# Token-tile steps interleaved at the joints of a fused two-block transformer kernel, one weight remainder moved to GpSimd, one clamp moved ahead of a split

## The reference

```python
ff = swiglu(rms_norm_2(h, g[0]), ffn_w_gate_up[i, 0], ffn_w_down[i, 0])
h = h + 0.5 * rms_norm_2(ff, g[1])
m_in = rms_norm_2(h, g[2])
mix = short_conv_mixer(...) if i == 0 else gated_deltanet_mixer(...)
h = h + rms_norm_2(mix, g[3])
ff = swiglu(rms_norm_2(h, g[4]), ffn_w_gate_up[i, 1], ffn_w_down[i, 1])
h = h + 0.5 * rms_norm_2(ff, g[5])
```

## Time and profile before

| | |
|---|---|
| median of three runs | 1706.47 us (1706.26 to 1706.6) |
| profiled execution: time | 1707.06 us |
| profiled execution: span, first to last instruction | 1705.1 us |
| mean granted TensorE clock | 0.963 of full |
| busy: TensorE, VectorE, ScalarE, GpSimd | 91%, 60%, 49%, 6% of the span |

### The profile page before, as it was taken

How to read it: one execution, slowest core, us unless ns; L and a number is a source line. 1 busy time by engine, 2 the same in 40 slices (tenths; PEclk the granted TensorE clock), 3 DMA queues, 4 the chain that set the end, 5 groups by cost and what they waited for, 6 DMA issues and landing times.

```text
span 1705.1 us, 19163 instructions
## 1 busy us (share of the span) xinstructions
PE 1554.3 (91%) x7536; PEld 1274.7 (75%) x7536; DVE 1022.7 (60%) x1345; ACT 832.8 (49%) x1174; POOL 96.0 (6%) x171
## 2 busy tenths in 40 slices
PE   4999889998999999899998999886688899989997
PEld 4777668777888778788877888764577778778886
DVE  3666566755665566666566565646655556766564
ACT  4535454463454454544455444554445645554443
POOL 4000000000000000000000000000422221000000
PEclk9899979999999999999999999988989999999999
DMA  4333433333555555555545555342322212455552
GB/s 157 121 98 124 123 100 114 99 121 109 191 186 184 173 181 177 164 184 183 191 158 182 179 192 191 123 132 72 87 56 75 75 50 75 154 163 189 192 179 99
DMA packets 165712, 238.77 MB, mean 140 GB/s; under 512 B 19358, under 2 KB 112328, under 8 KB 165624
## 3 DMA queue, kind: packets, MB, share of 16 engines
q1 hardware_dynamic: 154336, 230.98, 41.6%
q0 software_dynamic: 1632, 5.41, 1.1%
q10 hardware_dynamic: 9656, 1.18, 0.4%
HBM read 235.96 MB, written 1.57 MB: 139 GB/s over the span
## 4 chain that ended last, share of the span: by engine, by line
PE 70%; DVE 12%; ACT 8%; issue 5%; DMA 3%; POOL 1%; ACTq 1%; SPq 0%; DVEq 0%; POOLq 0%
PE A L226 12%; PE A L227 11%; PE A L228 11%; PE G L226 4%; PE G L228 4%; PE G L227 4%; PE M L228 4%; PE M L226 4%; PE M L227 4%; DVE w_lo L210 3%; ACT w_hi L197 2%; DVE gdn_gd_t L2274 2%; PE G L947 2%; PE G L989 1%; DMA raw<-in_w_mem_kv 1%
## 5 line engine op out<-in xcount | busy, mean ns | idle before, releaser
L210 DVE TENSOR_TENSOR w_lo<-raw,w_hi 128x2048 fp32r<-128x2048 f32 (+1 forms) x290 | 511.8, 1781 | 250.5 <-ACT w_hi L197 249.1
L197 ACT ACTIVATE w_hi<-raw 128x2048 fp32r<-128x2048 f32 (+1 forms) x290 | 424.5, 1483 | 206.6 <-DMA raw<-in_ffn_w_gate_up 151.5
L226 PE MATMUL A<-w_hi,x_hi 128*128 128x512 f32 (+3 forms) x688 | 291.9, 424 | 19.1 <-ACT gdn_gd_u L2048 9.6
L227 PE MATMUL A<-w_lo,x_hi 128*128 128x512 f32 (+3 forms) x688 | 270.6, 393 | 0.0
L228 PE MATMUL A<-w_hi,x_lo 128*128 128x512 f32 (+3 forms) x688 | 270.5, 393 | 0.0
L226 PEld LDWEIGHTS A<-w_hi,x_hi 128*128 128x128 f32 x688 | 138.8, 202 | 52.9 <-DVE x_lo L351 11.3
L228 PEld LDWEIGHTS A<-w_hi,x_lo 128*128 128x128 f32 x688 | 138.3, 201 | 27.8
L227 PEld LDWEIGHTS A<-w_lo,x_hi 128*128 128x128 f32 x688 | 138.9, 202 | 21.7 <-issue 2.4
L226 PE MATMUL A<-w_hi,ffn_ffn_hT_hi 128*128 128x512 f32 x352 | 139.9, 397 | 0.0
L227 PE MATMUL A<-w_lo,ffn_ffn_hT_hi 128*128 128x512 f32 x352 | 139.6, 397 | 0.0
L228 PE MATMUL A<-w_hi,ffn_ffn_hT_lo 128*128 128x512 f32 x352 | 138.2, 393 | 0.0
(11 more groups left out here) (348 smaller groups left out, 2263.7 us busy)
## 6 DMA issues: line engine op xcount, KB each, us to landing
raw<-in_ffn_w_gate_up SPq DMA_DIRECT2D x176, 512.0 KB, 4.8
raw<-in_ffn_w_down SPq DMA_DIRECT2D x88, 512.0 KB, 4.0
raw<-in_w_in SPq DMA_DIRECT2D x52, 512.0 KB, 4.6
raw<-in_gdn_w_in SPq DMA_DIRECT2D x48, 512.0 KB, 4.6
raw<-in_sc_w_in SPq DMA_DIRECT2D x24, 512.0 KB, 4.3
raw<-in_w_out SPq DMA_DIRECT2D x16, 512.0 KB, 4.5
raw<-in_gdn_w_out SPq DMA_DIRECT2D x16, 512.0 KB, 4.3
raw<-in_w_mem_kv SPq DMA_DIRECT2D x8, 512.0 KB, 8.2
```

Source lines behind the costliest of these rows:

```text
L197: ins = act.activation(net.w_hi[:, v % RING, part], net.raw[:, v % RING, part], ACT.Copy)
L210: ins = dve.tensor_tensor(net.w_lo[:, v % RING, part], net.raw[:, v % RING, part], net.w_hi[:, v % RING, part].bitcast(F32), ALU.subtract)
L226: pe.matmul(out, xh, hi[:, k, c, :], start=start and k == 0, stop=False)
L227: pe.matmul(out, xh, lo[:, k, c, :], start=False, stop=False)
```

## The change

Three edits.

1. At the joints VectorE takes the steps of the two token tiles in turn: after the first rest of tile 0 comes the add of x (1, 0), then the second rest, then the add of x (1, 1). `tmp` is shared, so the adds of tile 1 wait for the rests. ScalarE takes round 0, the squares of A3 and the root, and then rounds 1 to 3.
2. VectorE no longer makes the remainder of the second look-ahead unit (`leave_lo`). GpSimd makes it, in one instruction of 128x2048, when ScalarE's high part of that unit and the remainders before it are done (`pool_lo`). VectorE's next remainder waits for it. At the end of the last phase there is no such unit.
3. At the last step of each of the four FFNs ScalarE makes the sigmoid first and then the high part of the last unit; VectorE makes the clamp, then that unit's remainder, then the gate.

```diff
@@ Walk.split_lo
         dve.wait_ge(net.w_hi_ready, v + 1)
+        if self.left == v - 1:
+            dve.wait_ge(net.w_lo_ready, v)
         ins = dve.tensor_tensor(net.w_lo[:, v % RING, part], net.raw[:, v % RING, part],
                                 net.w_hi[:, v % RING, part].bitcast(F32), ALU.subtract)
@@
+    def leave_lo(self):
+        self.left, self.u = self.u, self.u + 1
@@ Post.act
         if then is not None:
             then.round(w, 0)
-            then.round(w, 1)
         self.squares(w, 1, 1)
         self.root(w, 1)
         if then is not None:
-            then.round(w, 2)
-            then.round(w, 3)
+            for n in range(1, 4):
+                then.round(w, n)
@@ Post.add (now for one tt and one c)
+        if tt == 1 and self.then is not None:
+            dve.wait_ge(*self.then.lo(c + 1))
@@ Post.dve
         w.split_lo()
-        self.add(w, 0)
-        if self.then is not None:
-            self.then.dve_tile(dve, 0)
-        w.split_lo()
-        self.add(w, 1)
-        if self.then is not None:
-            self.then.dve_tile(dve, 1)
+        w.leave_lo()
+        self.add(w, 0, 0)
+        self.add(w, 0, 1)
+        if then is not None:
+            then.gain(dve, 0)
+            then.gain(dve, 1)
+            then.rest(dve, 0)
+        self.add(w, 1, 0)
+        if then is not None:
+            then.rest(dve, 1)
+        self.add(w, 1, 1)
+        if then is not None:
+            for n in (2, 3):
+                then.gain(dve, n)
+            for n in (2, 3):
+                then.rest(dve, n)
+            dve.wait_ge(*then.lo(4))
         dve.wait_ge(*self.x_ready(4))
+
+    def pool_lo(self, pool):
+        net, v = self.net, self.end + 1
+        if v >= len(net.sizes):
+            return
+        n = net.sizes[v]
+        pool.wait_ge(net.w_hi_ready, v + 1)
+        pool.wait_ge(net.w_lo_ready, v)
+        pool.tensor_tensor(net.w_lo[:, v % RING, 0:n], net.raw[:, v % RING, 0:n],
+                           net.w_hi[:, v % RING, 0:n].bitcast(F32), ALU.subtract).then_inc(net.w_lo_ready, 1)
@@ Ffn.act, last step
+        w.split_hi()
+        self.hid_hi(w, self.steps - 2)
+        self.sigmoid(w, self.steps - 1)
+        w.split_hi()
         self.hid_hi(w, self.steps - 1)
@@ Ffn.dve, last step
+        w.split_lo()
+        self.hid_lo(w, self.steps - 2)
+        self.clamp(w, self.steps - 1)
+        w.split_lo()
+        self.gate(w, self.steps - 1)
         self.hid_lo(w, self.steps - 1)
```

More of the change, by code:

```diff
@@ L163, in __init__ @@
     def __init__(self, net, eng, chain_sem=None):
-        self.net, self.eng, self.u = net, eng, 0
+        self.net, self.eng, self.u, self.left = net, eng, 0, None
         self.chain = Chain(eng, chain_sem) if chain_sem is not None else None
@@ L352, in rest @@
                           ALU.subtract).then_inc(self.lo.sem, 1)
[L354 to L359, removed]
     def dve(self, w):
@@ L437, in act, with add @@
         if then is not None:
-            then.round(w, 2)
-            then.round(w, 3)
-    def add(self, w, tt):
+            for n in range(1, 4):
+                then.round(w, n)
+    def add(self, w, tt, c):
         dve, net = w.eng, self.net
-        dve.wait_ge(*self.r_ready(tt + 1))
-        if tt == 0:
+        if c == 0:
+            dve.wait_ge(*self.r_ready(tt + 1))
+        if (tt, c) == (0, 0):
             dve.wait_ge(*self.loaded(16))
[L446 to L454, removed]
+        if tt == 1 and self.then is not None:
+            dve.wait_ge(*self.then.lo(c + 1))
+        cols = slice(c * 512, (c + 1) * 512)
+        dve.scalar_tensor_tensor(out=net.tmp[:, c, :], in0=net.A[2 * tt + c][:, :],
+                                 scalar=net.post_r[:, tt:tt + 1], in1=net.brow[:, cols],
+                                 op0=ALU.mult, op1=ALU.mult).then_inc(self.scaled.sem, 1)
+        dve.wait_ge(*self.scaled(2 * tt + c + 1))
+        dve.scalar_tensor_tensor(out=net.x[:, tt, cols], in0=net.tmp[:, c, :],
+                                 scalar=self.scale, in1=net.x[:, tt, cols],
+                                 op0=ALU.mult, op1=ALU.add).then_inc(self.x_ready.sem, 1)
@@ L456, in dve @@
     def dve(self, w):
-        dve = w.eng
+        dve, then = w.eng, self.then
         w.split_lo()
-        self.add(w, 0)
-        if self.then is not None:
-            self.then.dve_tile(dve, 0)
-        w.split_lo()
-        self.add(w, 1)
-        if self.then is not None:
-            self.then.dve_tile(dve, 1)
-        dve.wait_ge(*self.x_ready(4))
+        w.leave_lo()
[5 more added lines that the diff above has]
+            then.rest(dve, 0)
@@ L507, in pool @@
         self.post.pool(pool)
+        self.post.pool_lo(pool)
     def sp(self, w):
@@ L600, in act @@
         self.sigmoid(w, 0)
-        for j in range(1, self.steps):
+        for j in range(1, self.steps - 1):
             w.split_hi()
@@ L605, in act @@
             self.sigmoid(w, j)
-            if j < self.steps - 1:
-                w.split_hi()
+            w.split_hi()
+        w.split_hi()
+        self.hid_hi(w, self.steps - 2)
+        self.sigmoid(w, self.steps - 1)
+        w.split_hi()
         self.hid_hi(w, self.steps - 1)
@@ L612, in make_hidden, with clamp @@
     def make_hidden(self, w, j):
+        self.clamp(w, j)
+        self.gate(w, j)
+    def clamp(self, w, j):
         net, dve = self.net, w.eng
@@ L620, in make_hidden, with gate @@
         ins.then_inc(self.clamped.sem, 1)
+    def gate(self, w, j):
+        net, dve = self.net, w.eng
         dve.wait_ge(*self.gated(j + 1))
```

## The result

| | before | after |
|---|---|---|
| median of four runs | 1706.53 us (1706.26 to 1708.65) | 1728.96 us (1725.98 to 1731.27) |
| ratio | | 1.0133 (95% interval 1.0112 to 1.0154) |
| span of the profiled execution | 1705.1 us | 1726.1 us |
| mean granted TensorE clock | 0.963 | 0.953 |
| busy: TensorE, VectorE, ScalarE, GpSimd (us) | 1554.3, 1022.7, 832.8, 96.0 | 1567.4, 1031.7, 831.5, 120.8 |

The changed kernel is 1.3% slower: 22.4 us by the medians, 21.0 us by the spans. In its lines the remainder on VectorE is L212, the adds are L449 and L453, gains L353, rests L358, transpositions L328 and L567, and GpSimd's remainder is L488.

A forecast was written before the change was run, and what follows sets the result against it. The prediction took TensorE's work plus its stands as the bound. FFN ends 4.2, joints 7.0 and clock 8.5 us sum to 19.7, added to the 1706.47 us median: 1726.2 us, range 1714 to 1733.

The forecast's parts named there:

- FFN ends, 4.2 us: Last hidden transposition of four FFNs: TensorE idle rises to 3.13 us each from 2.51, 1.83, 1.99, 2.02; 4.2 us added.
- The line of 6.94 us: FFN end: clamp, sigmoid, high part, remainder and what follows run one behind the other, 6.94 us in sum.
- GpSimd's instruction, 4.6 us: Joints: GpSimd's 128x2048 remainder takes 4.6 us, extrapolated from its 128x64 and 128x512 rows.
- Who waits: Joints: VectorE's second add, both inputs in SBUF, waits for GpSimd's earlier instruction, starting at 605.1 instead of 600.95.
- the single row of 1.49 us: Earlier trace: a two-SBUF-input VectorE instruction starting 0.35 us behind GpSimd took 1.49 us, against 0.69 for one of equal size.
- A joint, +1.39 us, 7.0 in all: Joints: third transposition at 610.97 against 609.58, so 1.39 us later at each, 7.0 us for five.
- The clock, 8.5 us: TensorE's low clock behind longer stands: 6.5 us at joints, 2.0 at FFN ends; 8.5 together, bounds 0 and 14.
- rival 2: Joints: GpSimd's instruction is longer; at 5.1 us with two low clock stretches at some joints, 1733 us; chance 0.12.
- All 13 idle times of 2.75 us and more are followed by a low stretch.: TensorE in the earlier trace, behind the start: every idle time this long was followed by half clock (0.50).
- Rival 1: Joints: VectorE's second add starts ahead of GpSimd and the first remainder waits; +0.4 us a joint, 1720.8 us; chance 0.12.
- Rival 3: Joints: GpSimd's long instruction does not block VectorE's second add; 1705.4 us, not slower; chance 0.07.
- Rival 4: FFN ends and joints: gate not held by the remainder, FFN stands and two low stretches vanish, joints gain; 1687 us; chance 0.04.

The follow-up runs named there:

- experiment 4: Joint edits only, FFN ends as before, with GpSimd also waiting until VectorE's second add is done; 1712.96 us against 1705.45 for the kernel before, ratio 1.0043.
- experiment 5: Joint edits only, with GpSimd's remainder cut into four instructions of 128x512; 1702.99 us against 1704.10 for the kernel before, ratio 0.9987.
- experiment 8: Joint edits only, with unread matmuls filling TensorE's two stands at each joint; 1709.46 us against 1704.10 for the kernel before, ratio 1.0023.
- experiment 2: Kernel before with only the FFN-end edit (both engines), joints as before; 1716.28 us against 1705.45, ratio 1.0063.
- experiment 9: FFN-end edit only, with 13 unread matmuls ahead of each last hidden transposition; 1707.74 us against 1704.27 for the kernel before, ratio 1.0024.
- experiment 3: Kernel before with only VectorE's half of the FFN-end edit, ScalarE keeping its old order; 1692.24 us against 1705.45, ratio 0.9924.
- experiment 1: Joint edits only, both engines' FFN ends as in the kernel before; 1718.57 us against 1705.45 for the kernel before, ratio 1.0077.

## Why the prediction was right, point by point

The forecast was 1726.2 us (19.7 more); the measured median is 1728.96 (22.4 more), in the range and the way forecast.

- *FFN ends, 4.2 us.* Idle was forecast at 3.13 us each and is 3.11 at all four; 4.1 us. The line of 6.94 us is 6.92 in the trace.
- *GpSimd's instruction, 4.6 us.* 4.55 in all five. The line through 128x64 and 128x512 held four times farther out.
- *Who waits.* The second L453, five times, 4.8 us; the single row of 1.49 us at the same distance was enough. Experiments 4 and 5 show it by moving and by cutting.
- *A joint, +1.39 us, 7.0 in all.* Experiment 8 has 5.8 us (1.16 a joint). The term was over by 0.2 us a joint. In experiment 8 the second transposition comes 7.06 us behind the first scaling, not 7.17 (605.94 less 598.77). The first unit comes 2.03 us behind it, not 1.98. From there it is 2.87 us to the third transposition, not the 3.05 that I took from the earlier trace rows: those reckon to the end of the last matmul, and without a stand the next instruction starts before that end.
- *The clock, 8.5 us.* This is the term that was mis-sized. At the joints I counted 1.3 us each, 6.5 in all; the trace after has 16.0 - 5.8 = 10.2. The step that failed is the count of low stretches, one for each joint: at three of the five joints the low level lasts 6.7 us (606.3 to 613.0 and its like), twice the 3.3 of the other two. Set against experiment 8, the two joints with the short one are 1.2 and 1.5 us longer, as I had counted, and the three with the long one 2.4 to 2.7. That a part of a low stretch falls on idle time held: TensorE is busy for 5.47 of those 6.70 us. Two low stretches at some joints stand in the prediction only under rival 2. At the FFN ends I counted 2.0; the profiled execution has low stretches behind two of the four ends, as before, and 0.9 us for all that lies outside the stands and joints, while experiments 2 and 9 together have about 7, with the doubt said there.
- *The sum.* Of the 21.0 us between the spans I had 19.7: 3.7 too little for the clock at the joints, 1.2 too much for the wait there, 1.1 too much for the rest and 0.1 for the stands. That the last three give back most of the first is luck. The two mechanisms, who waits for whom at the joints and the one line at the FFN ends, are not.
- *"All 13 idle times of 2.75 us and more are followed by a low stretch."* Behind the start the trace before has 12 of these, not 13; the thirteenth ends the start itself (5.19 us, at 20.5), and no low stretch follows it. The rule did not hold after: of four stands of 3.11 us two are followed (ffn00, ffn10), two are not (891.6 to 895.0 is at 1.00). In gdn three more of 2.85 to 3.29 us are not. In experiment 2 all four FFN ends are followed. So the rule was too strict, and one trace is no measure of how often it holds.
- *Rivals.* Rival 1 was built by hand in experiment 4 and costs 7.5 us, three quarters of what it would have been given (14.3 less the FFN's 4.2 is 10.1). Rivals 3 and 4 fall: L453 does not go through, and ScalarE's order holds the gate. Rival 4's price (stands and low stretches at the FFN ends gone, 11.6 us) is what experiment 3 reaches, 13.2, once ScalarE's order is left alone.

What stays open: which stretches outside the edited parts run at the low clock. Gdn, untouched in all kernels, was between 393.1 and 398.6 us long in the profiled executions. Nothing here shows what decides that, and it limits what a median of a few runs can say to some 2 us.

## What to carry to other kernels

Follow each moved instruction to the engine that feeds it: the clamp ahead of the remainder pays only if the remainder's own input is not queued behind the clamp's reader. Before work goes to GpSimd, list VectorE's instructions with two SBUF inputs that start while it runs, and give GpSimd several short instructions rather than one long one. And do not price a new stand of TensorE by its wait alone: at the joints here, with stands of 2.6 and 1.4 us, the wait was worth 5.8 us and the clock behind it 9.4.

## What the runs showed of the hardware that I had not expected

- The clock's share was larger than the wait's: 9.4 us against 5.8 at the joints (experiment 8 against experiment 1). For the FFN edit it is about 7 against 4 by the medians (experiment 9 against experiment 2), in part in gdn and not at the FFN ends.
- Equal stands are not followed by equal clocks: 3.11 us was followed by 0.50 for 3.3 us, for 6.7 us, or not at all.
- Matmuls whose result nobody reads, put into a stand, take 9.4 us off the five joints and 7.7 off the median, with the wait itself unchanged (L453 4.83 us against 4.79).
- The blocking goes both ways: four GpSimd instructions of 128x512 take 5.91 us beside VectorE, where four undisturbed ones would take 5.1 by the 1.28 us of the earlier trace rows, and one of 128x2048 takes 4.55 with VectorE standing.
